# Two transformer blocks on one core: attention 2 reordered, first weights in two halves, tables behind the input

## The reference, cut to what matters

```python
def reference(x, ...):
    x = first_block(x, ...)       # 8 forget-gated heads + 8 sparse heads, relu^2 feed-forward, norm
    return second_block(x, ...)   # 16 meta tokens ahead of x

# second_block, what the change touches
hn = rms_norm_2(h, attn_norm_g)
aq, ak, av, bq, bkv, iq, ik, iw, gates = split(hn @ w_in)
gate_a, gate_b = split(sigmoid(gates + b_gates))
o_a = sliding_window_sink_attention(aq, ak, av, sinks, bias_a)        # 8 heads, window 128 + meta
o_b = indexed_sparse_mla(q_abs, c_kv, iq, ik, iw, w_uv, bias_b)       # 8 heads, top-k keys
mixed = gate_a * (o_a @ w_branch_a) + gate_b * (o_b @ w_branch_b)
h = h + mixed @ w_out
```

## Time and profile before

| | us |
|---|---|
| median of 3 runs | 1539.82 |
| lowest and highest | 1535.42, 1544.96 |
| the profiled execution | 1541.67 |
| its span | 1539.9 |
| TensorE busy | 1502.4 (98%) |
| VectorE, ScalarE, GpSimd busy | 1003.8, 668.6, 351.7 |

### The profile page before, as it was taken

One profiled execution on the slowest core, in us unless ns is written; L12 is line 12 of the kernel. 1 busy time (PEld: TensorE's weight loads), 2 busy tenths in 40 slices (PEclk: granted clock), 3 DMA queues, 4 the chain that ended last, 5 costly groups with the idle time before them and its releaser, 6 DMA issues.

```text
span 1539.9 us, 21888 instructions
## 1 busy us (share of the span) xinstructions
PE 1502.4 (98%) x8094; PEld 1235.7 (80%) x8098; DVE 1003.8 (65%) x1917; ACT 668.6 (43%) x1180; POOL 351.7 (23%) x367
## 2 busy tenths in 40 slices
PE   7999989999999999999999999999999999999997
PEld 5787556788887989899887788766678889889887
DVE  4657676444457859686867787587275677568444
ACT  5533577322245434343456433566344333333232
POOL 3300455100020000000055544445432210120112
PEclk9999899999999999999999999999999999999999
DMA  5663100422222322332232564312322323322221
GB/s 198 133 161 123 42 15 1 136 96 96 96 96 83 110 96 96 101 106 96 93 107 69 165 163 113 117 49 83 137 96 82 109 83 115 105 96 97 97 95 56
DMA packets 47849, 154.28 MB, mean 100 GB/s; under 512 B 5842, under 2 KB 8082, under 8 KB 47744
## 3 DMA queue, kind: packets, MB, share of 16 engines
q1 hardware_dynamic: 43008, 137.63, 26.9%
q0 software_dynamic: 4736, 15.25, 4.5%
HBM read 142.78 MB, written 9.55 MB: 99 GB/s over the span
## 4 chain that ended last, share of the span: by engine, by line
PE 89%; DVE 6%; ACT 2%; issue 2%; DMA 0%; another core or an unknown queue 0%; SPq 0%; DVEq 0%; POOL 0%; ACTq 0%
PE PSA L702 72%; PE PSA L918 5%; PE PSA L917 5%; PE PSA L916 5%; PE PSA L986 2%; DVE WL L1999 1%; PE PSA L1130 1%; DMA XT<-xT_in 0%; ACT WH L1494 0%; DVE AR L2193 0%; DVE AHL L2286 0%; ACT AHL L1625 0%; ACT AR L1576 0%; DVE Al L1999 0%; DVE AR L2027 0%
## 5 line engine op out<-in xcount | busy, mean ns | idle before, releaser
L702 PE MATMUL PSA<-Ah,WH 128*128 128x512 f32 x1072 | 422.5, 394 | 9.8 <-DVE Al L2007 8.9
L702 PE MATMUL PSA<-Ah,WL 128*128 128x512 f32 x1072 | 418.5, 390 | 0.0
L702 PE MATMUL PSA<-Al,WH 128*128 128x512 f32 x1072 | 418.4, 390 | 0.0
L1999 DVE TENSOR_TENSOR WL<-WR,WH 128x1024 fp32r<-128x1024 f32 (+2 forms) x191 | 239.9, 1256 | 87.7 <-ACT WH L1494 87.5
L1494 ACT CAST WH<-WR 128x1024 fp32r<-128x1024 f32 (+3 forms) x218 | 225.1, 1034 | 116.9 <-PE PSA L702 55.7
L702 PEld LDWEIGHTS PSA<-Ah,WH 128*128 128x128 f32 x1072 | 201.9, 188 | 57.9 <-issue 14.7
L702 PEld LDWEIGHTS PSA<-Ah,WL 128*128 128x128 f32 x1072 | 201.9, 188 | 42.5
L702 PEld LDWEIGHTS PSA<-Al,WH 128*128 128x128 f32 x1072 | 202.1, 188 | 41.7 <-issue 0.7
L2850 POOL TENSOR_TENSOR AR<-AR 128x512 f32<-128x512 f32 (+1 forms) x44 | 55.5, 1272 | 570.8 <-ACT AR L1512 570.0
L3012 POOL TENSOR_TENSOR AR<-AR 128x512 f32<-128x512 f32 x22 | 47.4, 2155 | 267.4 <-DVE AR L2765 267.4
L916 PE MATMUL PSA<-ARR,WH 128*128 128x256 f32 x352 | 99.6, 283 | 0.0
(11 more groups left out here) (418 smaller groups left out, 2839.6 us busy)
## 6 DMA issues: line engine op xcount, KB each, us to landing
WR<-w_in SPq DMA_DIRECT2D x228, 512.0 KB, 3.3
gt_tmp<-AR SPq DMA_DIRECT2D x16, 256.0 KB, 2.2
WR<-w_in SPq DMA_DIRECT2D x8, 384.0 KB, 3.0
XT<-scr_tmp POOLq DMA_DIRECT2D x8, 264.0 KB, 5.1
XT<-scr_tmp POOLq DMA_DIRECT2D x8, 256.0 KB, 15.1
XT<-xT_in POOLq DMA_DIRECT2D x1, 2048.0 KB, 9.2
x_tmp<-XT POOLq DMA_DIRECT2D x1, 2048.0 KB, 7.7
AHL<-gt_tmp SPq DMA_DIRECT2D x8, 256.0 KB, 3.8
```

Of the source, the lines that this page charges most:

```text
L702: return pe.matmul(o, l, r, start=start, stop=stop)
L1999: dv.tensor_tensor(wl, x, wh.bitcast(F), ALU.subtract).then_inc(w_lo, 1)
```

## The change

Start: weight tile 0 is loaded and split in two halves of 512 columns (semaphores `d_w0`, `w_half`), the second load issued after input chunks 0 and 1. TensorE multiplies constants: `ones(9)` (nine float32 products of 256 columns, all of `ONE`) ahead of fq 0, `ones(2)` ahead of its chunk 1 and 2. GpSimd's table loads wait for the last piece of the input. Attention 2: the meta columns of pairs 2 and 3 are turned in bank 7, so that units 25 and 33 wait no longer for a copy; branch A's output 0 moves from step 46 to 47, its output 6 from 67 to 69, their gates on VectorE from 48 to 51 and 69 to 72; VectorE's low split of br2a 0 moves from 38 to 42. Merge 2: `sparse_part(4, (0, 1, 2))` comes first on TensorE; of the eight sums of both branches VectorE makes the last four (`joined`), and the order of splits and low parts changes.

```diff
+        d_w0, w_half = sem("d_w0"), sem("w_half")
...
-        g_sc = Sig(sem("g_sc"), ("gates", 16), ("sums", 8))
+        g_sc = Sig(sem("g_sc"), ("gates", 16), ("sums", 4))
-        m_dv = Sig(sem("m_dv"), (1, 24), ("a", 8), ("b", 8))
+        m_dv = Sig(sem("m_dv"), (1, 24), ("a", 8), ("b", 12))
...
+        def meta_place(pair):
+            return bank(7)[0:64, 0:128] if pair > 1 else bank(5)[0:64, 128:256]
...
-        A_AT = {46: 0, 55: 1, 63: 2, 64: 3, 65: 4, 66: 5, 67: 6, 71: 7}
+        A_AT = {47: 0, 55: 1, 63: 2, 64: 3, 65: 4, 66: 5, 69: 6, 71: 7}
-        GATED_AT = {48: 0, 57: 1, 65: 2, 66: 3, 67: 4, 68: 5, 69: 6, 73: 7}
+        GATED_AT = {51: 0, 57: 1, 65: 2, 66: 3, 67: 4, 68: 5, 72: 6, 73: 7}
+        LOW_AT = {42 if t == 36 else t + 2: name for t, name in SPLIT_AT.items()}
...
-            weights(0)
+            def first_half(e):
+                sp.dma_start(raw(0)[:, 512 * e:512 * e + 512], d["w"][0, :, 512 * e:512 * e + 512]).then_inc(w_ld[0] if e else d_w0, 16)
+            first_half(0)
             for k, n in X_LOADS:
+                if k == 2:
+                    first_half(1)
...
-                ws = halves_ready(j)
+                if j:
+                    ws = halves_ready(j)
+                else:
+                    pe.wait_ge(w_half, 2)
+                    ws = halves(0)
                 for k in range(nk):
+                    if j == 0 and k == 4:
+                        halves_ready(0)
...
             def merge2():
-                for o in range(4):
+                sparse_part(4, (0, 1, 2))
+                for o in range(5):
                     sparse_part(o, (3,))
-                for o in range(4, 8):
+                for o in range(5, 8):
                     sparse_part(o, (0, 1, 2, 3))
...
-                if i % 8 == 1 and 1 < i < 34:
+                if i % 8 == 1 and 1 < i < 18:
                     pe.wait_ge(r_mc, i // 8)
...
                 if i % 8 == 7 and x == "A":
-                    pe.transpose(bank(5)[0:64, 128:256], EMA[pair % 2], ident).then_inc(r_mt, 1)
+                    if pair == 2:
+                        pe.wait_ge(h_vm, 2)
+                    if pair == 3:
+                        pe.wait_ge(r_mc, 3)
+                    pe.transpose(meta_place(pair), EMA[pair % 2], ident).then_inc(r_mt, 1)
...
+            def ones(n):
+                for i in range(n):
+                    mm(bank(7)[:, 0:256], ONE[:, 0:1].to_broadcast([128, 128]), ONE[:, 0:1].to_broadcast([128, 256]), True, True)
+            ones(9)
-            feat(tid["fq", 0], hA, 8, bank(0), wait_norm("n1"))
+            feat(tid["fq", 0], hA, 8, bank(0), wait_norm("n1"), beside={1: lambda: ones(2), 2: lambda: ones(2)})
...
 # ScalarE, merge2
                 for k in range(8):
-                    ac.wait_ge(g_sc.sem, g_sc.at("sums", k))
+                    if k < 4:
+                        ac.wait_ge(g_sc.sem, g_sc.at("sums", k))
+                    else:
+                        ac.wait_ge(m_dv.sem, m_dv.at("b", 2 * k - 3))
                     high(2, k)
-                    if k in (2, 5):
-                        split_to(tid["wo2", k // 2])
+                    if k in (1, 4):
+                        split_to(tid["wo2", (k + 2) // 3])
...
 # VectorE, merge2
+            def joined(o):
+                dv.wait_ge(m_dv.sem, m_dv.at("b", 2 * o - 4))
+                dv.tensor_tensor(MG[:, o, :], MG[:, o, :], G2[o], ALU.add).then_inc(m_dv.sem, 1)
...
-                for k in range(3):
+                for k in range(2):
                     low(2, k)
                 for o in range(4, 8):
                     gated_b(o)
-                    low(2, o - 1)
+                    joined(o)
                     if o in (4, 6):
                         split_to(tid["wo2", o // 2 - 1])
-                low(2, 7)
+                    low(2, o - 2)
+                for k in (6, 7):
+                    low(2, k)
...
 # GpSimd
+            pl.wait_ge(d_x[-1], 16)
             pl.dma_start(TB, d["tab"]).then_inc(d_tab, 16)
...
-            for o in range(8):
+            for o in range(4):
                 pl.wait_ge(m_dv.sem, m_dv.at("b", o))
                 pl.tensor_tensor(MG[:, o, :], MG[:, o, :], G2[o], ALU.add).then_inc(g_sc.sem, 1)
```

More of the change, by code:

```diff
@@ L1132, in transposes2 @@
                 if i % 8 == 7 and x == "B":
[L1133 to L1138, removed]
+                    pe.wait_ge(r_mc, pair)
+                    if pair > 4:
                         pe.wait_ge(m_dv.sem, m_dv.at("a", pair - 5))
@@ L1735, in scalar_program @@
             ac.activation(NS[:, 24:25], ONE[:, 0:1], ACT.Square)
-            split_to(0)
-            ac.wait_ge(d_cst, 16)
+            split_at[0] = 1
             for k in range(8):
+                if k in (0, 2):
+                    ac.wait_ge(w_ld[0] if k else d_w0, 16)
+                    ac.copy(WH[0][:, 256 * k:256 * k + 512], WR[0][:, 256 * k:256 * k + 512]).then_inc(w_half if k == 0 else w_hi, 1)
+                if k == 0:
+                    ac.wait_ge(d_cst, 16)
                 ac.wait_ge(d_x[max(i for i in range(len(X_LOADS)) if X_LOADS[i][0] <= k)], 16)
@@ L2357, in attention2 @@
                                 dv.wait_ge(r_pv, pair - 1)
-                            dv.tensor_copy(PTMA[pair % 2][0:64, :], bank(5)[0:64, 128:256]).then_inc(r_mc, 1)
+                            dv.tensor_copy(PTMA[pair % 2][0:64, :], meta_place(pair)).then_inc(r_mc, 1)
                     if t - 1 in PROJ_AT:
@@ L2369, in attention2 @@
                         gated_a(GATED_AT[t])
-                    if t - 2 in SPLIT_AT:
-                        split_to(tid[SPLIT_AT[t - 2]])
+                    if t in LOW_AT:
+                        split_to(tid[LOW_AT[t]])
             def gated_a(o):
@@ L2445, in vector_program @@
             dv.tensor_copy(IDB[:, :], ident).then_inc(k_dv.sem, 1)
-            split_to(0)
+            split_at[0] = 1
             for k in range(8):
+                if k in (0, 2):
+                    dv.wait_ge(w_half if k == 0 else w_hi, 1)
+                    half = slice(256 * k, 256 * k + 512)
+                    dv.tensor_tensor(WL[0][:, half], WR[0][:, half], WH[0][:, half].bitcast(F), ALU.subtract).then_inc(
+                        w_half if k == 0 else w_lo, 1)
                 raw_low("n1", k, gv[0])
```

## The result

The changed kernel takes 1534.61 us (median of 22 runs, 1531.26 to 1539.05), the kernel before 1539.28 (22 runs, 1535.42 to 1547.54). The ratio is 0.9968 with an interval of 0.9957 to 0.998: 4.7 us are gained, by the interval 3.1 to 6.6. I had forecast 1532.1, 7.7 us less.

What follows compares the result with a forecast made beforehand. TensorE's stream of matmuls was taken as the bound; 2.1 + 0.4 + 0.4 + 0.5 + 0.8 + 3.3 + 0.4 = 7.9, less 0.2, gave 7.7 us and 1532.1 us. Range 1529 to 1535.5, with rivals 1525.5 to 1538.5.

Steps and rivals of the forecast that it cites:

- (1), (2), (4) constants: Start: constants end at 7.5 us, clock fast from then; chunk 2 at about 10.6, fq 0 ending near 14.8.
- Rival A: Start: constants don't raise the clock, chunk 2 comes at 14.6; only 2.3 us gained, 1537.5 us; chance 0.10.
- (3): Start: the rest of the input lands 1.1 us earlier (bounds 0 and 2.4), the tables no longer ahead.
- rival C: Everything lands: input 2.4 us earlier, start gives 3.4, step 47's wait shrinks; 10.0 gained, 1529.8 us; chance 0.14.
- (5): Start: TensorE can gain 1.1 + 1.1 = 2.2 us before waiting at the sums of squares; 2.1 taken.
- (6) to (9): Attention 2: 0.4 us at units 25 and 33, 0.4 for the split, 0.5 for output 0's gate, 0.8 for output 6.
- (7): Attention 2: split moved from step 38 to 42; its 0.76 us wait returns before output 0, saving 0.4.
- (10): Merge 2: nine of sixty products fill the 1.49 us gap, no pause lets the clock fall; 3.3 us saved.
- (11): Merge 2: VectorE's list holds with 1.9 us to spare, so 0.4 us of the wait for wo2 1 goes.
- rival B: Merge 2: VectorE becomes the bound, splits at 2.31, ending 2.5 us late; gain 5.2, 1534.6 us; chance 0.14.
- (D): Attention 2: the clock falls at step 47 and the change is slower; cost 25 us, 1557 us; chance 0.04.
- the 0.2 that I had set aside: Whole kernel: 0.2 us taken off the summed gain for waits of a tenth that appear when others go.

Runs made afterwards that it cites:

- no_ones: The changed kernel without the constants' products; the sums of squares begin at 26.67 us, 1.7 later than in the changed kernel.
- before_again: The kernel before, unchanged, profiled a second time; attention 2 takes 93.29 us, merge 2 28.25.
- tables_first: The changed kernel with GpSimd's three table loads issued at once again; sums of squares begin at 25.30 us against 24.96 in the changed kernel.
- merge_old: The changed kernel with merge 2 as in the kernel before; merge 2 takes 27.38 us against 26.85 in the changed kernel.
- merge_order: The changed kernel with VectorE's merge 2 list reordered (wo2 1 split right behind chunk 0's low part); merge 2 takes 25.70 us, 1.15 less.
- out0_46: The changed kernel with branch A's output 0 back at step 46 and its gate at 48; attention 2 takes 93.68 us.
- best_fill: The changed kernel with br2a 0's low split at step 39, merge_order's order and constants' products in block 1's waits; 1530.23 us, ratio to before 0.9947.

## Why the prediction was right, and which steps were not

The forecast was a gain of 7.7 within the range to 1538.5, and no change by more than one per cent: that held; the range is wide, though: its upper end is only 1.3 us below the 1539.82 that I started from. By its steps:

- **(1), (2), (4) constants.** Right: a fast clock from the first real product. Rival A fell, since the constants do raise the clock. What they are worth is the 1.7 of no_ones. A's own price stays untested: there slow constants would also have delayed the chunks, chunk 2 to 14.6, where no_ones has it at 11.34.
- **(3) the data.** I took 1.1 for the input that lands earlier; it was 0.56 in this pair of profiles and some 0.8 over eleven, within the bounds 0 to 2.4. No run shows a part of the tables in it; 0.7 comes of the half of tile 0, by one profile. The 173 GB/s that made me doubt (and rival C's ground) don't look like the tables' doing: from 4 to 6 us before_again moves 224 GB/s and tables_first 241, the changed kernel 250.
- **(5) what is late next.** The rule was right (TensorE waits when it has gained 1.1 plus what GpSimd gains) and 1.1 + 0.56 = 1.66 is what it allows; measured 1.60, of which 1.5 lasts. The start gave 1.5 for 2.1 forecast, by the size of (3): the mis-sized term is the 1.1.
- **(6) to (9) attention 2.** Undisturbed 2.2 instead of 2.1. Laid against the kernel before: 0.2 at unit 25, 0.2 at unit 33, 0.93 at step 38, of which the wait for output 0 at step 47 takes back all but 0.02, while 0.45 is left after it because unit 40 is turned earlier; then 0.60 for the gate, less 0.33 at 1065.6 (a new wait), and 1.03 for output 6. That is the forecast's mechanism in each place, the give-back of (7) too. The profiled execution shows only 1.0, since its clock fell at 1031.
- **(10) merge 2.** 3.3 forecast; from the end of attention 2 to the end of the sixty products 3.0 were gained between these two profiles. But 1.6 of it is a slow stretch of one execution, which I took for a property of the gap; without it this step is worth some 1.5. Against merge_old and before_again the changed merge gains 0.5 and 1.4 in all.
- **(11) the failed step.** "wo2 1 is split by 1122.0 in my order of the list": with attention 2 and the start 2.47 ahead that is 1119.5, and it was 1121.83. The term mis-sized is "eight low parts at 0.68": the first two took 3.48 together, 2.1 more than 1.36. The earlier trace rows had the answer, 1772 ns as the longest of that line. Instead of 0.4 gained, 0.4 is lost before wo2 and 0.5 inside, 1.3 against the forecast. So rival B came true in part: its sign, TensorE waiting for VectorE's split and low part, is there, at about half of its price of 2.5 and for another reason than its splits. The two splits of wo2 took 1.22 once GpSimd's four additions were over (2.31 for the first of them in the kernel before), which is what the Trainium skill (GPSIMD Engine Reference, Specifications), by which GpSimd shares its SBUF interface with VectorE's instructions of two SBUF inputs, led me to expect; I had applied it to the splits alone and not to the low parts. In merge_order the wait before wo2 is gone, so it is the order's, though there the split of wo2 1 takes 2.31 and the second low part 0.68.
- **(D) the clock in attention 2.** It did fall in some executions, but at 1031 in the profile after and at 1027 in tables_first, not at step 47 (there only in out0_46, after 1.97 us of waiting), and it cost 1.0 to 1.15, not 25. Of six profiles with the changed attention 2 four don't have it, nor have the two of the kernel before. Whether the edit makes it likelier stays open.

So the profiled gain came 3.1 below the forecast's 7.7: 0.6 at the start, 1.1 in attention 2 (the slow stretch), 1.6 in merge 2 (1.3 of it by (11)), less the 0.2 that I had set aside.

Two agreements are luck. The measured 1534.61 is rival B's 1534.6, but B put the whole shortfall of 2.5 into merge 2. And the two profiles differ by 4.6, as the medians do by 4.7, though each holds a slow stretch that the other lacks (1.6 us in merge 2 before, 1.15 in attention 2 after; in the first attention the clock was low for 13.7 us in both). Without slow stretches the parts are 1.5 at the start, 2.2 in attention 2, and 0.5 against merge_old or 1.4 against before_again in merge 2: 4.2 to 5.1, which is where the medians lie.

## What to carry to other kernels

Before one profile is explained, look at the granted clock in short stretches over the whole span: here a kernel's own executions differ by 8 us, and most of that goes with it, more than the change is worth. Compare stretches within an execution, and try constants' products in TensorE's pauses among small matmuls, as best_fill does. And when an engine's list is summed beside another engine's work, take the row's longest duration, not its median, for what runs beside it; then order the list by when TensorE needs each result.

## What the runs showed of the hardware

- In thirteen profiles without the fill the clock was low in the first attention for 0 (twice), 3.4 (twice), 6.8 (three times), 10.2, 13.7 (three times), 17.1 and 20.5 us, with identical code there. 20.5 went with 861.85 us for that part, 0 with 854.12 and 854.20. A slow us cost 0.10 to 0.43 us, depending on where it fell (0.10 in before_again, 0.34 in the kernel before, 0.38 with the 20.5; why so different isn't shown). No pause of TensorE there is longer than 1.1 us, and each fall lies inside, or at most 2.4 us behind, one of the pauses of 0.93 us (near 158 and 163), 1.11 us (near 195), or 0.70 and 0.57 us (near 224). best_fill puts its fifteen products of constants into these; the longest pause left there is 0.8 us, and its clock stays up. The Trainium skill (TensorE: Matmul & The Clock Gate, A second HAM failure mode: psum-queue depth-cycling) tells of a clock that oscillates when TensorE pauses briefly between groups of matmuls; these traces agree, with pauses of 0.6 to 1.1 us.
- At the very start products of 128x512 stand 0.43 us apart while the column PEclk says 1.00; at 1112 us the same spacing goes with 0.50. The column can't be read at the start.
- In merge 2 VectorE's instructions of two SBUF inputs and GpSimd's additions hold each other up, and the one that starts later pays. With 0.24, 0.56, 0.85 and 1.22 us left of an addition, a split or low part of VectorE takes 0.1, 0.4, 0.7 and 1.1 longer than its 1.22 or 0.68 (merge_old at 1112.16 and 1126.30, before at 1118.65, after at 1117.60). An addition that starts while a split runs takes 2.29 to 2.37 instead of 1.29. That is the difference between 1.32 and 2.29 for one split. VectorE's instructions with an input in PSUM (L2416) stay at 0.67 to 0.69 beside the same additions.
